# Six reorderings in a two-layer hybrid encoder on one core: refill steps, last-head order, last division on DVE, three weight buffers for the output projections, weights split ahead, scores ahead of transposes

## The chip, the cores and the metric

The kernel runs on one core of one Trainium2 chip. The metric is the device time of one execution in microseconds (us). An execution's time is a little longer than the span of its profile, which runs from the first to the last recorded instruction.

## The reference

Two layers over 1024 tokens of width 1024, all in float32. Layer 0 is a chunk-causal differential attention with eight heads and a squared-ReLU MLP; layer 1 is a sliding-window attention with shared keys and values and a second MLP of the same shape. Cut to what matters here:

```
def attend_block(args):                       # layer 0, for each block of 128 queries
    logits = einsum('bqhcd,bkhcd->bhcqk', q_blk, k) - slopes * dist      # two components c
    p = softmax(where(allowed, logits, -inf))
    wts = p[:, :, 0] - lam * p[:, :, 1]
    return einsum('bhqk,bkhe->bqhe', wts, v)
o = rms_norm(o, subln_g) * (1.0 - lambda_init)         # the division of each head's output
x = x + o @ w_o
x = x + (relu(rms_norm(x, g) @ w_up) ** 2) @ w_down
k, v = rms_norm((rms_norm(x, kv_norm_g) @ w_kv)[...])  # shared keys and values
# layer 1: 16 query heads in 4 groups, a window of two chunks of 64, a sink in each softmax
x = x + windowed_attention(rms_norm(x), k, v) @ w_o
x = x + (relu(rms_norm(x, g) @ w_up) ** 2) @ w_down
```

## The kernel before, in words

**Arithmetic.** Every float32 product is three reduced-precision products on TensorE (PE): high times high, high times low, low times high. So each operand is split once: ACT copies it, rounded, to the high part (`copy`, L952), and DVE subtracts that from the original for the low part (`low`, L1412, or L1413 with a gain). Whatever PE multiplies has gone through ACT and then DVE. Five instruction streams (PE, ACT, DVE, POOL and SP, which issues the DMAs) are written out by hand, each in its own order; semaphores hold them together, and no scheduler moves anything.

**Stages, in order of time.** 0 to 470 us: the first attention, a head at a time, with the projections of the next head between the steps. 470 to 543: its last head (`last_head`), which has no projections left. 543 to 636: the output projection, as eight panels of 128 output channels (`panel_products`; a panel's weights are split by `split_panel` on ACT and DVE, into `w_hi` and `w_lo`, which lie in `w_op`). 636 to 1264: the first MLP. 1264 to 1335: shared keys (job 0) and values (job 1). 1335 to 1563: second attention, four groups whose queries are projected as jobs 2 to 5. 1563 to 1597: the last steps of it, without projections. 1597 to 1686: second output projection. 1686 to 2334: second MLP.

**A step of the first attention.** A step `s` of a head handles 128 queries against 128(s+1) keys. DVE adds the distances and takes the maximum of both components (`maxima`, L1592, tile p) and writes their negative (`nm_a`, L1597); ACT takes both exponentials (`exps`, L1030); DVE forms the coefficient (L1606) and mixes the two (`mix`, L1611); PE transposes the weights into `trb`; ACT and DVE split them into `wT_hi` and `wT_lo`; PE multiplies by the values into `pv`. When all heads are done, outputs are normed per query (on POOL in `norm_steps`, with `chain_o` and `rstd_o`), transposed into oT, which lies in `xT`, and split into `a_hi` and `a_lo`. `EARLY = (7, 3)` says how many heads' outputs are split before the last head is done.

**The MLP.** A product of two 2x2 block matrices is done with seven block products instead of eight; their names are A11, S1, S2, A12, S3, A22, S4. One product takes 12 matmuls into one bank. Operands of x stay in `xop` and `a` (`unit_hi`, `unit_lo`), weights stream through `w_op` (`op_of_weights`, LEAD = 4 products ahead on DVE, 5 on ACT). In the second half (weights down) the operand of u comes back from DRAM: per slice of four outputs, 4 slices in a segment, 14 half-slots of `xop` are loaded (`load_at`) and split again (`refill_hi` on ACT, `refill_lo` on DVE); `refill_at(k)` says in which step of the product loop. `down_add` (L1694) adds a finished bank to `xT`, and frees it.

**The second attention.** Its weights are loaded and split per job (`wb_split` into `wb_hi`, `wb_lo`, eight rows of 128x256, all at a job's boundary). In a step PE transposes q (L2298), transposes the exponentials of the step before (L2315), takes scores (L1958) and multiplies; `Fori(1, KVH - 1)` loops over groups 1 and 2.

## Time and profile before

| what | before |
|---|---|
| time, median of 3 runs | 2344.01 us (2340.61 to 2346.03) |
| time of the profiled execution | 2336.36 us |
| its span | 2334.6 us |
| PE busy | 2213.6 us, 95% |
| DVE, ACT, POOL busy | 1595.2 us (68%), 1162.6 us (50%), 844.4 us (36%) |
| PE's part of the chain that ended last | 80%, DVE 10%, ACT 3% |

The span less the busy time of PE is 121 us, and PE has the largest share of the chain. To see which of those 121 us an edit can touch, each stage is read by itself: windows of the span (busy time of each engine and PE's granted clock, as a share of full speed), PE's waits by what ended them, and the timeline of one engine, in which a square bracket at a row's end tells how long the engine stood idle ahead of it and what released it.

### The profile page before, as it was taken

To read this page: it belongs to the slowest core of one execution; us is meant where nothing else is said; L and a number is where in the kernel's file an instruction comes from. 1 tells how busy PE (TensorE), PEld (TensorE's weight loads), DVE (VectorE), ACT (ScalarE), POOL (GpSimd) and SP (SyncE) were. 2 spreads that over 40 slices of the span, in tenths; PEclk is the share of its full clock that TensorE was granted. 3 is DMA by queue.
4 is the path that set the end of the run, shared out by engine and by line. 5 is a ranking of instruction groups with operands and counts; after the bars stand their busy time and mean duration, and the time that the engine had idled before them with its cause. 6 is when DMAs were issued, how large, how long until landed. Compare 5 with 4: busy or idle time off the path is not lost.

```text
span 2334.6 us, 36548 instructions
## 1 busy us (share of the span) xinstructions
PE 2213.6 (95%) x11916; PEld 1901.1 (81%) x11916; DVE 1595.2 (68%) x3190; ACT 1162.6 (50%) x2484; POOL 844.4 (36%) x1464
## 2 busy tenths in 40 slices
PE   7999999967999999999999989998999999899998
PEld 6899999956878888778777988887878888778777
DVE  6788788763676666876776378874676666876773
ACT  5566666653555555543344256654555555543342
POOL 3333333334633322233344155553633322233331
PEclk9999999968999999999999999998999999999999
DMA  6111110002434444663352100003434445663352
GB/s 203 31 28 28 27 27 22 2 28 96 130 103 158 157 151 165 247 229 106 129 198 91 37 20 20 0 20 109 126 113 152 153 150 171 237 232 103 132 172 81
DMA packets 186628, 255.86 MB, mean 110 GB/s; under 512 B 14944, under 2 KB 135776, under 8 KB 181856
## 3 DMA queue, kind: packets, MB, share of 16 engines
q1 hardware_dynamic: 186464, 253.82, 32.8%
q8 instruction: 86, 1.41, 0.3%
q14 instruction: 78, 0.64, 0.1%
HBM read 174.09 MB, written 79.69 MB: 109 GB/s over the span
## 4 chain that ended last, share of the span: by engine, by line
PE 80%; DVE 10%; issue 4%; ACT 3%; DMA 1%; POOLq 1%; POOL 0%; DVEq 0%; SPq 0%; ACTq 0%
PE score L1958 45%; PE trb L1958 13%; PE proj L1958 13%; PE pv L1958 5%; DVE xop L1412 3%; DVE w_op L1412 1%; PE trb L1999 1%; PE trb L2315 1%; ACT p L1030 1%; DVE xT L1694 1%; DVE p L1592 1%; DMA w_quad<-in_mlp_w_down 1%; DVE pb L1905 1%; DVE wb_lo L1413 1%; ACT pb L1377 1%
## 5 line engine op out<-in xcount | busy, mean ns | idle before, releaser
L1958 PE MATMUL score<-xop,w_op 128*128 128x512 f32 x3840 | 893.6, 391 | 24.0 <-DVE xop L1412 12.9
L1958 PEld LDWEIGHTS score<-xop,w_op 128*128 128x128 f32 x3840 | 720.9, 189 | 183.6 <-issue 34.5
L828 POOL TENSOR_TENSOR w_quad<-w_quad,w_sum 128x512 f32<-128x512 f32 x64 | 99.6, 1557 | 806.9 <-DVE w_op L1412 806.9
L1958 PE MATMUL trb<-xop,w_op 128*128 128x512 f32 x1536 | 361.8, 390 | 5.7 <-DVE w_op L1412 1.7
L1958 PEld LDWEIGHTS trb<-xop,w_op 128*128 128x128 f32 x1536 | 287.5, 188 | 68.9 <-issue 6.3
L952 ACT ACTIVATE w_op<-w_quad 128x512 fp32r<-128x512 f32 (+1 forms) x336 | 216.3, 646 | 246.6 <-PE score L1958 167.5
L1412 DVE TENSOR_TENSOR w_op<-w_quad,w_op 128x512 fp32r<-128x512 f32 (+1 forms) x336 | 284.3, 850 | 45.5 <-ACT w_op L952 45.5
L1694 DVE TENSOR_TENSOR xT<-score,xT 128x512 f32<-128x512 f32 x160 | 110.0, 687 | 158.5 <-PE score L1958 150.0
L1958 PE MATMUL score<-a_hi,w_op 128*128 128x512 f32 x512 | 160.8, 394 | 3.8 <-DVE w_op L1412 3.8
L1030 ACT ACTIVATE p<-p,nm_a,slopes 128x128 f32<-128x128 f32 (+7 forms) x124 | 106.5, 861 | 112.8 <-DVE nm_a L1597 110.7
L1412 DVE TENSOR_TENSOR xop<-xop 128x1024 fp32r<-128x1024 f32 x112 | 142.5, 1284 | 14.3 <-ACT xop L952 14.3
L952 ACT ACTIVATE quad<-score 128x512 f32<-128x512 f32 x96 | 57.3, 597 | 186.8 <-PE score L1958 178.2
L1958 PE MATMUL proj<-wa_hi,a_hi 128*128 128x384 f32 x418 | 142.8, 342 | 0.8 <-DVE v_parts L1413 0.8
L1958 PE MATMUL proj<-wa_hi,a_lo 128*128 128x384 f32 x418 | 140.0, 335 | 0.0
L1958 PE MATMUL proj<-wa_lo,a_hi 128*128 128x384 f32 x418 | 139.7, 334 | 0.0
L952 ACT ACTIVATE w_op<-w_sum 128x512 fp32r<-128x512 f32 x128 | 77.0, 627 | 107.7 <-PE score L1958 50.8
L1694 DVE TENSOR_TENSOR quad<-trb,quad 128x512 f32<-128x512 f32 x64 | 44.2, 690 | 110.0 <-PE trb L1958 76.1
L952 ACT ACTIVATE xop<-xop 128x1024 fp32r<-128x1024 f32 x112 | 115.7, 1046 | 5.4 <-DMA xop<-u_dram 5.4
L1958 PEld LDWEIGHTS score<-a_hi,w_op 128*128 128x128 f32 x512 | 97.5, 190 | 24.9 <-DVE w_op L1412 4.3
L471 POOL TENSOR_TENSOR chain_p<-rstd_qk 128x8 f32<-128x8 f32 x96 | 19.9, 208 | 245.7 <-DVE rstd_qk L463 236.3
L1592 DVE CUSTOM_DVE_ANT_0 p<-score,dist_a 128x128 f32<-128x128 f32 (+7 forms) x124 | 88.7, 752 | 29.2 <-PE score L1958 29.2
L1958 PE MATMUL proj<-wb_hi,b_hi 128*128 128x256 f32 x320 | 98.2, 307 | 6.8 <-DVE wb_lo L1413 5.8
(285 smaller groups left out, 4564.2 us busy)
## 6 DMA issues: line engine op xcount, KB each, us to landing
xop<-u_dram SPq DMA_DIRECT2D x112, 512.0 KB, 5.6
u_dram<-quad SPq DMA_DIRECT2D x32, 1536.0 KB, 9.6
w_quad<-in_mlp_w_up SPq DMA_DIRECT2D x64, 512.0 KB, 5.5
w_quad<-in_mlp_w_down SPq DMA_DIRECT2D x64, 512.0 KB, 4.9
wa_raw<-in_a_w_qkv SPq DMA_DIRECT2D x96, 128.0 KB, 2.5
quad<-xT_dram SPq DMA_DIRECT2D x32, 256.0 KB, 4.1
xT_dram<-xs SPq DMA_DIRECT2D x32, 256.0 KB, 2.6
u_dram<-quad SPq DMA_DIRECT2D x32, 256.0 KB, 3.8
```

The source lines that it names most:

```text
L828: return pool.tensor_tensor(out, x, y, ALU.subtract)
L952: return nc.scalar.activation(out, in_, ACT.Copy, scale=scale)
L1030: nc.scalar.activation(p[:, 0:keys], p[:, 0:keys], ACT.Exp, bias=nm_a[i][:, c:c + 1], scale=one(slopes, h), accum_out=ssum[par][:, c, s:s ...
L1377: nc.scalar.activation(pb[par][:, j, lo:256], pb[par][:, j, lo:256], ACT.Exp, bias=nm_b[par][:, j:j + 1], accum_out=sm_b[par][:, j:j + 1])
L1412: return nc.vector.tensor_tensor(out, full, hi.bitcast(F32), ALU.subtract)
L1413: return nc.vector.scalar_tensor_tensor(out=out, in0=full, scalar=scale, in1=hi.bitcast(F32), op0=ALU.mult, op1=ALU.subtract)
L1592: nc.vector.tensor_tensor_reduce(out=p[:, 0:keys], in0=score[c][:, 0:keys], in1=dist_a[:, S - keys:S], scale=1.0, scalar=LOWEST, op0=ALU.a ...
L1694: return nc.vector.tensor_tensor(out, a, b, ALU.add)
L1905: nc.vector.tensor_tensor_reduce(out=pb[par][:, j, lo:256], in0=score_cols(j, lo), in1=bias_b[:, j, lo:256], scale=1.0, scalar=LOWEST, op0 ...
L1958: return nc.tensor.matmul(out, a, b, start=start, stop=stop, **kw)
L1999: last = nc.tensor.transpose(trb[b][:, P * (kc - 4 * i):P * (kc - 4 * i + 1)], p0[block_s % 2][:, P * kc:P * (kc + 1)], ident[:, :])
L2315: last = nc.tensor.transpose(trb[b][:, P * j:P * (j + 1)], pb[s % 2][:, j, P * b:P * (b + 1)], ident[:, :])
```

## The change

1. Refills: the list of steps, of whose 14 entries the first three stay and eleven go one product earlier; in the loop over products both refills go to the head, on ACT ahead of all else in a step, on DVE right behind `down_add`.
2. Last head: each component's maximum is announced by itself, ACT starts the first exponential behind the first; ACT's `wT_hi` of a step goes ahead of the next exponentials; the panel splits and the squares move, and the low parts of seven heads' outputs go from POOL to DVE, behind the head.
3. The last division: nine small instructions and one multiply, on DVE instead of POOL.
4. Panels: three buffers and three pairs of PSUM banks instead of two, splits one panel further ahead; the early products of panels 0 and 1 first with `a_hi` alone; the last panel half by half.
5. `wb_split` in pieces, six of eight rows ahead of the job's boundary (odd jobs in other memory, `wb_rows`).
6. Second attention, steps without projections (`full` false): PE's scores ahead of the transposes of the weights, DVE's maxima ahead of their low parts.
7. The loop over groups 1 and 2 is written out.

```
-    steps = (1, 2, 4, 5, 6, 7, 8, 8, 9, 10, 11, 11, 12, 13)
+    steps = (1, 2, 4, 4, 5, 6, 7, 7, 8, 9, 10, 10, 11, 12)
...
+        w_hi = [w_op[:, i, :, :].rearrange("p a (k n) -> p (a k) n", n=P) for i in (2, 0, 5)]
+        w_lo = [w_op[:, i, :, :].rearrange("p a (k n) -> p (a k) n", n=P) for i in (3, 1, 6)]
...
+        wo_bank = [bank[0], bank[1], [proj[:, :], pv[:, :]]]
...
+        def rsqrt_steps_dve(dve, out, vec, t, n):
+            v, t = vec[:, 0:n], t[:, 0, 0:n]
+            for i in range(3):
+                if i:
+                    dve.drain()
+                dve.scalar_tensor_tensor(out=t, in0=v, scalar=-0.5, in1=out, op0=ALU.mult, op1=ALU.mult)
+                dve.drain()
+                dve.tensor_tensor(t, t, out, ALU.mult)
+                dve.drain()
+                last = dve.scalar_tensor_tensor(out=out, in0=t, scalar=1.5, in1=out, op0=ALU.add, op1=ALU.mult)
+            return last
...
+        def wb_rows(part, k, job):
+            if job % 2 and k < 6:
+                return wo_b[:, k // 2, part, 256 * (k % 2):256 * (k % 2 + 1)]
+            return (wb_hi, wb_lo)[part][:, k, :]
...
-            pool.wait_ge(qkv_ready, NH * NB)
-            split_early(0)
-            pool.wait_ge(o_rstd, NH)
-            norm_steps(rstd_o[:, :], chain_o, NB)
-            o = head_out[1]
-            pool.tensor_tensor(o, o,
-                               rstd_o[:, :].unsqueeze(2).to_broadcast([P, NB, P]), ALU.mult).then_inc(o_normed, 1)
...
+                def last_exps(s):
+                    keys, i = P * (s + 1), s % 2
+                    act.sem_inc(act_passed, 1)
+                    for c, p in ((0, p0[i]), (1, p1s[i])):
+                        act.wait_ge(nm_ready, h * NB + 2 * s + c + 1)
+                        nc.scalar.activation(p[:, 0:keys], p[:, 0:keys], ACT.Exp, bias=nm_a[i][:, c:c + 1],
+                                             scale=one(slopes, h),
+                                             accum_out=ssum[par][:, c, s:s + 1]).then_inc(exp_done, 1)
...
+                last_exps(0)
+                high_wT(uses, 0)
+                for s in range(NB - 1):
+                    high_wT(uses, s + 1)
+                    last_exps(s + 1)
...
+            high_early(5)
+            act.drain()
             square_outputs(NH * 4, 1, NB - 2)
+            high_early(6)
+            split_panel(2)
...
                 for k in range(OPS + 6):
+                    for s, h in refill_at(k):
+                        refill_hi(s, h)
...
                         op_of_weights(k + LEAD + 1)
-                    for s, h in refill_at(k):
-                        refill_hi(s, h)
...
+                def both_maxima(s):
+                    for c in range(2):
+                        if c:
+                            dve.wait_ge(mixed, h * NB + max(s - 1, 0))
+                        one_maximum(s, c)
...
+            dve.wait_ge(o_normed, NH - 1)
+            dve.drain()
+            rsqrt_steps_dve(nc.vector, rstd_o[:, :], chain_o, chain_p, NB)
+            dve.drain()
+            nc.vector.tensor_tensor(head_out[1], head_out[1],
+                                    rstd_o[:, :].unsqueeze(2).to_broadcast([P, NB, P]), ALU.mult).then_inc(o_normed, 1)
+            for c in range(EARLY[0]):
+                dve.wait_ge(o_early_hi, c + 1)
+                low(a_lo[:, c, :], oT[:, c, :], a_hi[:, c, :]).then_inc(o_split, 1)
+            split_panel(2)
...
+                    for s, h in refill_at(k):
+                        refill_lo(s, h)
                     if k < 4:
...
+                    full = proj_on and (s < NB - 1 or more)
+                    def low_weights_b():
+                        for b in range(2):
+                            if ("p", s, b) in uses:
+                                dve.wait_ge(bm_hi[b], uses["p", s, b] + 1)
+                                low(wTb_lo[:, b, :], trb[b][:, :], wTb_hi[:, b, :]).then_inc(bm_free[b], 1)
+                    if full:
+                        low_weights_b()
...
+                    pe.wait_ge(o_early_hi, k + 1)
+                    for i in range(2):
+                        x_h = a_hi[:, k, HALF * i:HALF * (i + 1)]
+                        mm(wo_bank[slot][i], w_hi[slot][:, k, :], x_h, k == 0, False)
+                        mm(wo_bank[slot][i], w_lo[slot][:, k, :], x_h, False, False)
+                    if slot and k == 2:
+                        transpose_outputs(last_uses, NH, 1)
+            for slot in range(2):
+                for k in range(EARLY[0]):
                     pe.wait_ge(o_split, k + 1)
-                    panel_products(slot, a_hi, a_lo, k)
-                if slot == 0:
-                    transpose_outputs(last_uses, NH, 1)
+                    for i in range(2):
+                        mm(wo_bank[slot][i], w_hi[slot][:, k, :], a_lo[:, k, HALF * i:HALF * (i + 1)], False, False)
 ...
-                    if i >= 2:
-                        pe.wait_ge(xs_ready, 16 * seg + 2 * i - 2)
+                    if i >= 3:
+                        pe.wait_ge(xs_ready, 16 * seg + 2 * i - 4)
+                    if i == KC - 1:
+                        last_panel(i % 3)
...
+            def last_panel(slot):
+                out, w_h, w_l = wo_bank[slot], w_hi[slot], w_lo[slot]
+                for k in range(KC):
+                    last = three(out[1], (w_h[:, k, :], w_l[:, k, :]), (a_hi[:, k, HALF:S], a_lo[:, k, HALF:S]),
+                                 k == 0, k == KC - 1)
+                last.then_inc(panel_half, 1)
+                for k in range(KC):
+                    mm(out[0], w_h[:, k, :], a_hi[:, k, 0:HALF], k == 0, False)
+                    last = mm(out[0], w_l[:, k, :], a_hi[:, k, 0:HALF], False, False)
+                    if k in (3, KC - 1):
+                        last.then_inc(wo_half, 1)
+                for k in range(KC):
+                    last = mm(out[0], w_h[:, k, :], a_lo[:, k, 0:HALF], False, k == KC - 1)
+                last.then_inc(panel_half, 1)
...
+                        if s in (2, 3, 4, NB - 2) and more:
+                            wb_split(g + 3, 4, *((6, KC) if s == NB - 2 else (2 * s - 4, 2 * s - 2)))
...
-            with act.Fori(1, KVH - 1) as g:
+            for g in range(1, KVH - 1):
...
+                    if not full:
+                        transpose_weights_b()
```

The order of instructions on ACT in the last head, before, around its seventh step's exponentials (p_0 and p are the two components of step 6, p_1 and p_last those of step 7, `w_op` a panel's weights, `sq_a` squares):

```order
L1030 ACTIVATE p_0,ssum<-p_0,nm_a,slopes 128x896
L1030 ACTIVATE p,ssum<-p,nm_a,slopes 128x896
L1139 ACTIVATE sq_a,oss<-oraw 128x128 x2
L952 ACTIVATE wT_hi<-trb 128x512
L952 ACTIVATE wT_hi<-trb 128x256
L952 ACTIVATE w_op<-w_quad 128x1024
L952 ACTIVATE a_hi<-xT 128x1024
L1030 ACTIVATE p_1,ssum<-p_1,nm_a,slopes 128x1024
L1030 ACTIVATE p_last,ssum<-p_last,nm_a,slopes 128x1024
L952 ACTIVATE wT_hi<-trb 128x512
L952 ACTIVATE wT_hi<-trb 128x384
```

The same place in the changed kernel:

```order
L1078 ACTIVATE p_0,ssum<-p_0,nm_a,slopes 128x896
L1078 ACTIVATE p,ssum<-p,nm_a,slopes 128x896
L969 ACTIVATE a_hi<-xT 128x1024
L1172 ACTIVATE sq_a,oss<-oraw 128x128 x2
L969 ACTIVATE w_op<-w_quad 128x1024
L969 ACTIVATE wT_hi<-trb 128x512
L969 ACTIVATE wT_hi<-trb 128x384
L1078 ACTIVATE p_1,ssum<-p_1,nm_a,slopes 128x1024
L1078 ACTIVATE p_last,ssum<-p_last,nm_a,slopes 128x1024
```

The weights of step 6 (the `wT_hi` of 384 columns) are now split ahead of step 7's exponentials and no longer behind them.

On DVE in the first slice of refills (`xT` is a `down_add`, `w_op` a weights' low part, `xop` a refill's), before:

```order
L1694 TENSOR_TENSOR xT<-score,xT 128x512
L1412 TENSOR_TENSOR w_op<-w_quad,w_op 128x512
L1412 TENSOR_TENSOR xop<-xop 128x2x512
L1694 TENSOR_TENSOR xT<-trb,xT 128x512
L1694 TENSOR_TENSOR xT<-score,xT 128x512
L1412 TENSOR_TENSOR w_op<-w_quad,w_op 128x512
L1412 TENSOR_TENSOR xop<-xop 128x2x512 x2
```

and in the changed kernel:

```order
L1772 TENSOR_TENSOR xT<-score,xT 128x512
L1458 TENSOR_TENSOR xop<-xop 128x2x512 x2
L1458 TENSOR_TENSOR w_op<-w_quad,w_op 128x512
L1772 TENSOR_TENSOR xT<-trb,xT 128x512
L1772 TENSOR_TENSOR xT<-score,xT 128x512
L1458 TENSOR_TENSOR xop<-xop 128x2x512
L1458 TENSOR_TENSOR w_op<-w_quad,w_op 128x512
```

A refill's low part now stands ahead of the weights' low part of its step, and the pair stands one product earlier, ahead of the two `down_add` of the next product.

On DVE in a step without projections (`mx_b` are the maxima, `wTb_lo` the weights' low part, `osb` the outputs of the step before), before:

```order
L1933 TENSOR_TENSOR osb<-osum,rc_b 128x256
L1412 TENSOR_TENSOR qTb_lo<-score,qTb_hi 128x256
L1412 TENSOR_TENSOR wTb_lo<-trb,wTb_hi 128x512 x2
L1905 ISA pb,mx_b<-score,bias_b 128x192
L1905 ISA mx_b 128x1
```

and in the changed kernel the end of the same step:

```order
L2000 TENSOR_TENSOR mx_b<-mx_b,sinks 128x4
L2002 TENSOR_TENSOR esin_b<-sinks,mx_b 128x4
L2003 TENSOR_SCALAR nm_b<-mx_b 128x4
L1458 TENSOR_TENSOR wTb_lo<-trb,wTb_hi 128x512 x2
L2015 TENSOR_TENSOR den_b<-sm_b,es_b 128x4
```

The weights' low parts went from ahead of the maxima to behind them.

## Rows read from the trace of the kernel before

**Rows 1.** Page, part 1: busy us, share of the span, instructions of each engine.

```profile
PE 2213.6 (95%) x11916; PEld 1901.1 (81%) x11916; DVE 1595.2 (68%) x3190; ACT 1162.6 (50%) x2484; POOL 844.4 (36%) x1464
```

**Rows 2.** Windows: length, then busy PE, PEld, DVE, ACT, POOL; PEclk, DMA share, GB/s.

```profile
470.00:543.00 73.00, 45.72 (x230) 36.56 (x229) 46.26 (x101) 34.81 (x83) 28.65 (x42) 0.63 0.15 44
935.00:977.00 42.00, 36.46 (x152) 28.72 (x151) 35.75 (x45) 27.89 (x41) 9.71 (x6) 0.96 0.79 288
1303.00:1315.00 12.00, 10.24 (x73) 10.07 (x72) 6.02 (x21) 4.98 (x13) 1.50 (x6) 0.86 0.21 65
```

**Rows 3.** Timeline of DVE, last head: start, length, instruction, [idle before, releaser].

```profile
477.63 0.35 DVE L1611 SCALAR_TENSOR_TENSOR p<-p,coef_a,p 128x128 f32<-128x128 f32 x1
...
523.83 1.21 DVE L1592 CUSTOM_DVE_ANT_0 p<-score,dist_a 128x1024 f32<-128x1024 f32 x1
...
529.65 1.16 DVE L1412 TENSOR_TENSOR wT_lo<-trb,wT_hi 128x512 fp32r<-128x512 f32 x2 [2.60 <-ACT wT_hi L952]
530.97 1.23 DVE L1412 TENSOR_TENSOR w_op<-w_quad,w_op 128x1024 fp32r<-128x1024 f32 x1 [0.17 <-ACT w_op L952]
...
533.44 2.22 DVE L1611 SCALAR_TENSOR_TENSOR p<-p_last,coef_a,p 128x1024 f32<-128x1024 f32 x1
```

**Rows 4.** Timeline of ACT, last head's step 7.

```profile
526.58 1.24 ACT L1030 ACTIVATE p<-p,nm_a,slopes 128x1024 f32<-128x1024 f32 x1 [6.30 <-DVE nm_a L1597]
...
529.05 0.95 ACT L952 ACTIVATE wT_hi<-trb 128x512 fp32r<-128x512 f32 x2
```

**Rows 5.** Timeline of DVE, the last mix of the head before.

```profile
470.18 1.28 DVE L1611 SCALAR_TENSOR_TENSOR p<-p,coef_a,p 128x1024 f32<-128x1024 f32 x1
```

**Rows 6.** Timeline of PE, first panels of the output projection.

```profile
569.17 0.53 PE L1958 MATMUL score<-a_hi,w_op 128*128 128x512 f32 x1 [3.83 <-DVE w_op L1412]
```

**Rows 7.** The chain that ended last, in order of time: start, length, work.

```profile
569.17 69.87 PE score L1958 x300
...
668.95 13.60 PE score L1958 x60
```

**Rows 8.** Timeline of PE, start of each MLP.

```profile
643.61 7.32 PE L1958 MATMUL score<-xop,w_op 128*128 128x512 f32 x24 [1.85 <-issue]
...
1711.25 3.00 PE L1958 MATMUL trb<-xop,w_op 128*128 128x512 f32 x12 [1.73 <-DVE w_op L1412]
```

**Rows 9.** PE's waits, 640 to 1264 us: total us, times, longest.

```profile
PE score L1958 <- DVE xop L1412: 6.5, 4, 3.2
```

**Rows 10.** Timeline of DVE, two refills' low parts of the second slice.

```profile
1031.58 1.22 DVE L1412 TENSOR_TENSOR xop<-xop 128x1024 fp32r<-128x1024 f32 x1
...
1035.68 2.32 DVE L1412 TENSOR_TENSOR xop<-xop 128x1024 fp32r<-128x1024 f32 x1
```

**Rows 11.** Page, part 6, DMA issues: count, KB each, us to landing.

```profile
xop<-u_dram SPq DMA_DIRECT2D x112, 512.0 KB, 5.6
```

**Rows 12.** PE's waits, 1290 to 1345 us, then 1345 to 1563.

```profile
PE pv L1958 <- DVE wb_lo L1413: 1.8, 1, 1.8
PE proj L1958 <- DVE wb_lo L1413: 1.6, 1, 1.6
...
PE proj L1958 <- DVE wb_lo L1413: 4.2, 3, 1.4
```

**Rows 13.** PE's waits, 1563 to 1598 us.

```profile
PE trb L2315 <- ACT es_b L1379: 5.9, 3, 2.3
...
PE score L1958 <- DVE qTb_lo L1412: 2.0, 1, 2.0
```

**Rows 14.** Timeline of PE, two steps in the loop and the same two in group 3.

```profile
1467.60 1.22 PE L2315 MATMUL trb<-ident,pb 128*128 128x128 f32 x8 [1.26 <-DVE kTb_lo L1413]
...
1481.08 1.09 PE L2315 MATMUL trb<-ident,pb 128*128 128x128 f32 x8 [0.51 <-ACT es_b L1379]
...
1528.70 1.22 PE L2315 MATMUL trb<-ident,pb 128*128 128x128 f32 x8 [1.06 <-DVE kTb_lo L1413]
...
1542.07 1.09 PE L2315 MATMUL trb<-ident,pb 128*128 128x128 f32 x8 [0.39 <-ACT es_b L1379]
```

More of the change, by code:

```diff
@@ L1199, in squares @@
                 def squares(i):
-                    for half in range(2):
+                    if i == KC - 1:
+                        act.wait_ge(panel_half, 2 * KC * (seg + 1))
+                    for half in halves_of(i):
                         if i % 2 and i < KC - 1:
@@ L1830, in segment @@
                         factors()
-                    for s, h in refill_at(k):
-                        refill_lo(s, h)
                     if seg == 0:
@@ L2383, in _ @@
             steps(0, False, True, range(NB))
-            with pe.Fori(1, KVH - 1) as g:
+            for g in range(1, KVH - 1):
                 steps(g, True, True, range(NB))
```

281 lines of the change are left out of this document (152 added, 129 removed).

## The prediction

> **What bounds the kernel now.** First the page's busy times: PE works 2213.6 us, 95% of the span, and DVE, the next, 68% [rows 1]. Outside of PE's own work only 2334.6 - 2213.6 = 121 us are left, and a part of PE's busy time is stretched by a lower clock. Then windows, to find where those lie [rows 2]. In the last head PE is busy 45.7 of 73 us at a mean granted clock of 0.63: it waits there for a circle of other engines. In a slice of refills (935 to 977) it stands 42 - 36.5 = 5.5 us, at 0.96; around the boundary of jobs (1303 to 1315) 1.8 us, at 0.86. The reader is to see that a stop costs twice: the idle time, and a time behind it in which the clock is down. I price each stage by its own waits and its own clock.
>
> The sum is made against the profiled execution, 2336.4 us; the median of the runs shown is 7.6 us above it, and I add that at the end.
>
> **A. Last head: 15 us.** From the end of the first mix (477.63 + 0.35 = 477.98) to the end of the last (533.44 + 2.22 = 535.66) seven steps take 57.7 us [rows 3]. This is a circle mix, maxima, exponentials, weights' split, coefficient, mix. What leaves it:
> - The second maximum. The first of step 7 ends at 523.83 + 1.21 = 525.04 [rows 3]; ACT starts the exponential at 526.58, having waited for nm_a, the two maxima's common result [rows 4]. 1.5 us, of which I take 1.15, since the announcement itself stays. It grows with the number of keys (0.34 in step 1), and over seven steps sums to 5.2.
> - Weights' split behind the exponentials. wT_hi runs at 529.05 [rows 4], wT_lo 529.65 to 530.8, and the coefficient can't start before [rows 3]. Summed over the steps 8.5 us. As the split goes ahead of the exponentials, PE's transposes and wT_hi enter the circle there, partly beside the first maximum: I take 3 back, so 5.5.
> - One of the two panel splits (the 1.23 at 530.97 of step 7; in the new order that of step 7 stays and the other goes behind the loop) 1.3, and squares on ACT 1.5.
> - POOL beside DVE. The mix over 1024 columns takes 2.22 in the last head [rows 3] and 1.28 in the head before [rows 5]; POOL was making the low parts of the seven outputs there, and these move behind the head. 0.94 for this one; with the smaller excesses of the other mixes, coefficients and low parts in the head I estimate 4.3.
>
> That is 17.8. PE's transposes run here at the low clock and gain a place in the circle, so I take 2 to 3 off: 15, bounds 10 and 19.
>
> **B. Join to the panels: 5.7 us.** At 569.17 PE waited 3.83 us for the low part of panel 2's weights [rows 6], since two buffers only let its split begin late. With three buffers it stands ahead of that. Behind the stop 300 matmuls took 69.87 us; at 13.60/60 = 0.2267 each they would take 68.0 [rows 7], so 1.9 more. The division on DVE I cost at nothing. Its cover is the 56 matmuls of panels 0 and 1 with high parts alone, 12.7 us at 0.2267; seven low parts are then wanted behind it, which DVE can begin some 6 us after the last values are there (my estimate from nine steps of a quarter microsecond and a multiply of 1.2), and takes 7 x 1.2 = 8.4 for. They come at about 557, the last is wanted at about 559: 2 us are left. If the cover were gone, each microsecond of lateness would be one of the end.
>
> **C. Starts of the MLPs: 6 us.** In the first, PE stood 1.85 us and then took 7.32 for 24 matmuls, where 24 x 0.2267 = 5.4 would do [rows 8]; with a further 0.5 stop some 4.0. In the second the same 1.85, 0.2, and 1.73 for a weights' low part [rows 8]: 3.7. The last panel's new order lets the operands be split half by half ahead of its end. It also puts four weights' low parts of DVE ahead of the second half's addition, so of 7.7 I take 6; bounds 2 and 7.7.
>
> **D. Refills: 11 us.** The waits for a refill's low part are 6.5 us in the first MLP, in four stops, the longest 3.2 [rows 9], and the same in the second, plus 0.8. The window 935 to 977 is the first slice: 5.5 us of stops and 0.04 x 42 = 1.7 of clock [rows 2]. There ACT's refill stood behind a weights' split whose own load came late; ahead of it, it doesn't wait. I take 4.5 of 7.2 for each MLP's first slice, 9. In the other three slices a refill's low part takes 1.22 or 2.32, the second when POOL works beside it [rows 10]. Two such in one step now stand ahead of the next product's additions into xT, which free PE's bank: 2 x 2.32 = 4.6 us against a product of 12 x 0.2267 = 2.7, so the bank comes about 1.9 late, where the old order waited 1.6. So those slices give little, 2 of some 6.6 in all. Together 11; bounds 4 and 18 (nothing in slice 0 beyond the one long stop; everything).
>
> The trace has that same row as evidence for the price of POOL's neighbourhood, 2.32 against 1.22 [rows 10]. The Trainium skill, page "SBUF — State Buffer", section "Who interferes with whom", says more: a DVE instruction with both inputs in SBUF contends with a GpSimd instruction that reads SBUF, and the loser waits for the whole of the other's instruction. A refill's low part has both inputs in SBUF, a low part from PSUM has not. By it every refill that meets a weights' sum of POOL would be doubled, and D would fall to its lower bound, 4; by the row, only those that the new place brings there, and D is 11.
>
> **E. Weights split ahead: 9 us.** PE waits for wb_lo 1.8, 1.6 and three times 1.4: 7.6 us [rows 12]. Clock behind the stops: 0.14 x 12 = 1.7 at 1303 to 1315 [rows 2], 0.9 at another by the same reading. Two rows of eight still are split at the boundary, and take some 1 back. What pays: steps 2 to 4 get two rows each, on ACT and DVE, which have room there. Sum 9; bounds 6 and 10.2.
>
> **F. Steps without projections: 2 us lost.** PE's transposes waited 5.9 us for the exponentials with the scores queued behind them [rows 13], which looks as though scores ahead would win. But the scores waited 2.0 for qTb_lo as well [rows 13], and the next step's exponentials hang on maxima that gain at most 0.5 to 1.3 once. Against it the weights' low parts now stand behind four maxima, with pv behind them, and this in four steps. Bounds: gain 0.5, loss 3.
>
> **G. The loop written out: 0.** The same two steps take 1481.08 - 1467.60 = 13.48 us in the loop and 1542.07 - 1528.70 = 13.37 straight [rows 14].
>
> Sum: 15 + 5.7 + 6 + 11 + 9 - 2 + 0 = 44.7. 2336.4 - 44.7 = 2291.7, and with 7.6 the median is **2299**. A measurement of this kernel tells 0.2%, 4.7 us, from no change.
>
> **The rivals.**
> - *The refills' waits only move* (chance 0.18). By the 2.32 row, refills at the head of the queue meet POOL and hold the additions. D gives nothing, or 1: 44.7 - 10.7 = 34, time 2310. For it: that row, and three slices whose bank comes late by my own working. Against: POOL is busy only 9.7 of 42 us in a slice [rows 2].
> - *PE at the low clock bounds the last head* (0.1). With other waits gone, PE's pair, outputs and weights transposes at 0.63 of the clock set the steps; A gives 7.5 less, time 2307. For it: 0.63 in 73 us [rows 2], and that PE stands 27 us of them. Against: if the head gets shorter, PE is busier in it. The Trainium skill, "TensorE: Matmul & The Clock Gate", section "What's actually happening", says that "the default state is throttled, and activity releases the throttle": by it a denser head would raise the clock and A would near 19.
> - *Everything in full* (0.2): 17.8 + 5.7 + 7.7 + 17 + 10.2 and nothing lost in F is 58.4, time 2286. For it: each is the trace's own wait. Against: waits of a chain seldom vanish without another that stood 1 to 2 us behind.
> - *Slower* (0.03). One mechanism: refills at the head of ACT's and DVE's queues wait for their own load. A load lands 5.6 us after issue [rows 11] and is now wanted 2 products, 5.4 us, after it, eleven of fourteen times. Each late microsecond then holds DVE's additions, and so PE. With 56 refills per MLP in pairs, 56 pairs in all: 1 us late each costs 56, and D's 11 isn't won: 33.7 - 56 = -22, time 2366. The turning point is 33.7/56 = 0.6 us per pair. Against: PE needs the freed bank two products later, and weights are split four products ahead, 10.9 us, which covers several such waits.
>
> **How the numbers follow.** The main case, 2292 to 2306, gets 0.4, the four rivals 0.51, and 0.09 is for mixtures with a gain of 10 to 30 us or of more than 60. Likeliest is 2299. The range from 2279 to 2320 takes in "in full" (2286) with the bounds of the terms beneath it, and 2310 with a further 10 for a lost C and F. Faster by over 0.2%: 0.95; within 0.2%: 0.02; slower: 0.03.
>
> **What would show it.** A: the mixes of steps 1 to 7 apart by 50 us less some (42.7 in place of 57.7), the last mix about 1.3 us long, the exponential beginning right behind the first maximum. B: no row of PE waiting for w_op after the join, and no wait for a_lo ahead of the 28 late matmuls. C: stops ahead of the MLPs' first products under 1 us. D: in 935 to 977 less than 3 us idle; in the later slices xop rows of 2.32 and PE waiting for DVE's xT. E: no waits for wb_lo above 0.5. F: PE waiting for wTb_lo or expb over 2 us in the steps without projections. The prediction is wrong if the head's steps hang on something I left out (PE's outputs of head 6 inside the circle), or if loads reach the head of ACT's queue late.

## The result and the profile after

The changed kernel takes 2310.8 us (median of 4 runs, 2306.0 to 2314.2), the kernel before 2342.3 beside it: a ratio of 0.9865, interval 0.9835 to 0.9895, so 1.35% or 31.5 us faster. The profiled execution took 2313.9 us, near the top of that spread, with a span of 2312.1; the profiled execution of before, 2336.4, lies below the median of its runs. So between the two profiles lie 22.5 us and not 31.5, and the ledger below is made of those 22.5.

The page, part 1 of the changed kernel, answers to [rows 1]; then the groups of part 5 for the refills on ACT and on DVE (busy, mean ns, idle before and what ended it), and their loads from part 6, which answer to [rows 11]:

```profile
PE 2205.3 (95%) x11916; PEld 1899.8 (82%) x11916; DVE 1603.9 (69%) x3215; ACT 1159.5 (50%) x2484; POOL 819.6 (35%) x1433
...
L1458 DVE TENSOR_TENSOR xop<-xop 128x1024 fp32r<-128x1024 f32 x112 | 145.8, 1317 | 11.4 <-ACT xop L969 11.2
...
L969 ACT ACTIVATE xop<-xop 128x1024 fp32r<-128x1024 f32 x112 | 116.9, 1052 | 72.5 <-DMA xop<-u_dram 72.3
...
xop<-u_dram SPq DMA_DIRECT2D x112, 512.0 KB, 5.8
```

PE still is busy 95% of a shorter span. What is new is the third row: ACT stands 72 us ahead of the refills for their loads, where it stood 5 before, though a load lands in 5.8 us where it did in 5.6.

Stretches between the same instructions of both profiles show where the time went (for the first row the end of a mix, for the others the start of a row of PE):

| stretch | before | after | gain | the prediction's term |
|---|---|---|---|---|
| last head, first mix to last mix | 57.7 | 39.2 | 18.5 | A 15 |
| last mix to PE's last product of the head | 3.5 | 3.2 | 0.3 | |
| to the MLP's third group of products | 122.3 | 114.4 | 7.9 | B 5.7 and C's 4.0 |
| first MLP, to the first product of keys | 610.6 | 617.6 | -7.0 | D |
| keys, values, groups 0 to 3 with projections | 270.0 | 258.8 | 11.2 | E 9, G 0 |
| steps without projections | 54.9 | 59.3 | -4.4 | F -2 |
| second panels, to the same place of the second MLP | 114.3 | 114.3 | 0.0 | C's second part |
| second MLP, to the transposes of the outputs | 616.8 | 620.3 | -3.6 | D |

The first of these stretches begins 0.5 us later than before; 22.9 - 0.5 is the 22.5 us between the spans, but for rounding. Each gain is that of one profile. Where the experiments run the same code in a stretch, their profiles give its spread, and this is told beside the term below.

**Last head.** The timeline of DVE after: the first mix, the first maximum of step 7, the last mix. They answer to [rows 3].

```profile
478.11 0.35 DVE L1658 SCALAR_TENSOR_TENSOR p<-p,coef_a,p 128x128 f32<-128x128 f32 x1
...
510.20 1.22 DVE L1679 CUSTOM_DVE_ANT_0 p<-score,dist_a 128x1024 f32<-128x1024 f32 x1
...
516.36 1.28 DVE L1658 SCALAR_TENSOR_TENSOR p<-p_last,coef_a,p 128x1024 f32<-128x1024 f32 x1
```

The mix takes 1.28 us where it took 2.22, and begins 6.2 us after the maximum, where it was 9.6. ACT's timeline, which answers to [rows 4]: the exponential now begins behind the weights' split, with no idle time, and not right behind the first maximum, as the prediction had it.

```profile
511.14 0.95 ACT L969 ACTIVATE wT_hi<-trb 128x512 fp32r<-128x512 f32 x2
511.99 1.23 ACT L1078 ACTIVATE p<-p,nm_a,slopes 128x1024 f32<-128x1024 f32 x1
```

PE's windows from the first mix to the head's last product, before and then after, show the clock (the column behind POOL) risen from 0.58 to 0.77:

```profile
478.00:539.00 61.00, 36.69 (x170) 28.36 (x168) 40.05 (x81) 31.70 (x73) 28.07 (x40) 0.58 0.11 35
```

```profile
478.00:521.00 43.00, 30.86 (x175) 25.39 (x175) 35.59 (x90) 30.95 (x72) 8.88 (x27) 0.77 0.06 18
```

**Join and division.** DVE's timeline, the last division's multiply, then the low parts (a row groups overlapping ones); and PE's first product with one of them, which has no bracket:

```profile
527.77 1.23 DVE L1757 TENSOR_TENSOR oraw<-oraw,rstd_o 128x1024 f32<-128x1024 f32 x1
528.92 3.49 DVE L1458 TENSOR_TENSOR a_lo<-xT,a_hi 128x1024 fp32r<-128x1024 f32 x3
```

```profile
536.48 6.51 PE L2049 MATMUL score<-a_lo,w_op 128*128 128x512 f32 x28
```

PE asks at 536.5 for what DVE began at 528.9, and has no stop between 520.9 and 623.9: the 3.83 us of [rows 6] are gone. At the MLPs' starts a wait for a weights' low part stays, which answers to [rows 8]:

```profile
635.21 3.00 PE L2049 MATMUL trb<-xop,w_op 128*128 128x512 f32 x12 [1.35 <-DVE w_op L1458]
...
1685.21 4.57 PE L2049 MATMUL trb<-xop,w_op 128*128 128x512 f32 x12 [2.01 <-DVE w_op L1458]
```

In the second row 12 matmuls take 4.57 us instead of 3.00. These 1.6 us of lower clock, right behind a stop of 2.0, fall into the second MLP's row of the table, though no refill has run yet.

**Refills.** All engines in the second slice of the first MLP, after (it answers to [rows 10]):

```profile
1005.23 1.06 ACT L969 ACTIVATE xop<-xop 128x1024 fp32r<-128x1024 f32 x1 [3.57 <-DMA xop<-u_dram]
...
1006.32 4.54 DVE L1458 TENSOR_TENSOR xop<-xop 128x1024 fp32r<-128x1024 f32 x2 [0.78 <-ACT xop L969]
...
1007.62 2.16 POOL L843 TENSOR_TENSOR w_quad<-w_quad 128x512 f32<-128x512 f32 x1
...
1010.79 1.76 DVE L1458 TENSOR_TENSOR w_op<-w_quad,w_op 128x512 fp32r<-128x512 f32 x1
...
1012.47 0.68 DVE L1772 TENSOR_TENSOR xT<-trb,xT 128x512 f32<-128x512 f32 x1
...
1013.07 0.68 DVE L1772 TENSOR_TENSOR xT<-score,xT 128x512 f32<-128x512 f32 x1
```

```profile
1013.85 11.53 PE L2049 MATMUL score<-xop,w_op 128*128 128x512 f32 x37 [3.67 <-issue]
```

To be read from above: ACT stands 3.57 us for a load, and DVE waits 0.78 of these for ACT; the two low parts take 4.54 us together, where two of 1.22 would take 2.4, since POOL is at work; the weights' low part behind them takes 1.76 where it takes 0.69 without POOL; only then come the two additions that free PE's banks, and PE starts 0.1 us after the second. The bracket says "issue" because the profile saw nothing end the wait, but the time points to the addition. There are six stops of this kind, of 2.4 to 3.7 us, in slices 2 to 4 of the two MLPs, where before each slice had one of 0.5 and one of 1.1.

Whether such a stop is of 2.4 us or of 3.6 hangs on who starts first. Here POOL's sum into `w_sum` began 0.07 us ahead of DVE's first low part. At the next slice DVE began 0.03 us ahead of the same sum:

```profile
1006.25 1.29 POOL L857 TENSOR_TENSOR w_sum<-w_quad 128x512 f32<-128x512 f32 x1
```

```profile
1089.13 3.47 DVE L1458 TENSOR_TENSOR xop<-xop 128x1024 fp32r<-128x1024 f32 x2 [0.69 <-ACT xop L969]
...
1089.16 2.35 POOL L857 TENSOR_TENSOR w_sum<-w_quad 128x512 f32<-128x512 f32 x1
```

There the two low parts took 3.47 us and PE stood 2.43. In all 42 such stops, six in each of seven profiles with these refills, it is so: with the sum ahead the stop is of 3.59 us or more, with DVE ahead of 2.36 to 2.45.

And a window of the slice of the 3.67 us stop:

```profile
1010.00:1092.00 82.00, 78.33 (x333) 64.47 (x333) 54.03 (x71) 29.87 (x42) 22.53 (x16) 0.96 0.41 137
```

0.04 x 82 = 3.3 us more, at the lower clock behind the stop.

**Second attention.** From 1290 to 1545 no wait for wb_lo is left, where [rows 12] had five. In the steps without projections, PE's timeline, which answers to [rows 13], and then DVE and POOL at the same place:

```profile
1540.82 0.36 PE L2049 MATMUL score<-kTb_hi,qTb_hi 64*128 64x192 f32 x2 [2.60 <-DVE qTb_lo L1458]
...
1545.48 0.45 PE L2049 MATMUL pv<-vb,wTb_hi 128*128 128x128 f32 x1 [2.38 <-DVE wTb_lo L1458]
...
1553.67 0.54 PE L2049 MATMUL score<-kTb_hi,qTb_hi 64*128 64x192 f32 x2 [3.66 <-DVE qTb_lo L1458]
```

```profile
1544.06 1.27 DVE L1458 TENSOR_TENSOR wTb_lo<-trb,wTb_hi 128x512 fp32r<-128x512 f32 x2
...
1545.19 2.35 POOL L804 TENSOR_TENSOR a_lo<-xT,a_hi 128x1024 fp32r<-128x1024 f32 x1
1545.26 2.30 DVE L2015 TENSOR_TENSOR den_b<-sm_b,es_b 128x4 f32<-128x4 f32 x1
```

The transposes lost their waits for es_b, but the scores wait for qTb_lo now, and pv 2.38 us for the low parts that went behind the maxima.

The stretch of keys, values and groups, 258.8 us here, takes 258.7 to 264.6 us in ten other profiles with the same code in it. The difference to the changed kernel's own profile lies mostly in PE's clock while the keys are made: 0.83 in their first 20 us here, 0.57 in e1 and before. Windows of this stretch, before, after, and in e1:

```profile
1272.09:1542.07 269.98, 248.56 (x2088) 236.54 (x2089) 184.04 (x672) 139.05 (x459) 120.12 (x429) 0.96 0.07 24
```

```profile
1252.82:1511.62 258.80, 240.71 (x2089) 229.43 (x2089) 186.06 (x672) 139.01 (x459) 122.56 (x429) 0.99 0.08 25
```

```profile
1250.62:1513.58 262.96, 245.67 (x2088) 234.11 (x2088) 185.69 (x672) 139.02 (x459) 122.53 (x429) 0.96 0.07 25
```

At the clock of before, 0.96, the gain is 7.0 us and not 11.2.

### The profile page after: what moved, and what is told of

It reads as the page before. It is cut to its first block, busy times and chain, and to the rows that moved or that the text cites. A ratio compares the mean times of both kernels' runs of the same rounds, so it can differ in the third digit from the quotient of the medians.

```text
span 2312.1 us, 36311 instructions
## 1 busy us (share of the span) xinstructions
PE 2205.3 (95%) x11916; PEld 1899.8 (82%) x11916; DVE 1603.9 (69%) x3215; ACT 1159.5 (50%) x2484; POOL 819.6 (35%) x1433
## 4 chain that ended last, share of the span: by engine, by line
PE 76%; DVE 11%; issue 5%; DMA 3%; ACT 2%; DVEq 1%; POOLq 1%; POOL 0%; ACTq 0%; SPq 0%
PE score L2049 41%; PE proj L2049 13%; PE trb L2049 13%; PE pv L2049 6%; DMA xop<-u_dram 3%; DVE xop L1458 2%; DVE w_op L1458 2%; PE trb L2090 1%; DVE pb L1994 1%; PE trb L2428 1%; ACT p L1047 1%; DVE wTb_lo L1458 1%; ACT xop L969 1%; PE trb L2144 0%; DVE osum L2021 0%
## 5 line engine op out<-in xcount | busy, mean ns | idle before, releaser
L843 POOL TENSOR_TENSOR w_quad<-w_quad,w_sum 128x512 f32<-128x512 f32 x64 | 89.0, 1390 | 799.6 <-DVE w_op L1458 799.6
L1458 DVE TENSOR_TENSOR xop<-xop 128x1024 fp32r<-128x1024 f32 x112 | 145.8, 1317 | 11.4 <-ACT xop L969 11.2
L969 ACT ACTIVATE xop<-xop 128x1024 fp32r<-128x1024 f32 x112 | 116.9, 1052 | 72.5 <-DMA xop<-u_dram 72.3
L1047 ACT ACTIVATE p<-p,nm_a,slopes 128x128 f32<-128x128 f32 (+7 forms) x112 | 96.4, 862 | 90.0 <-DVE nm_a L1644 90.0
L2049 PE MATMUL score<-a_hi,w_op 128*128 128x512 f32 x384 | 114.4, 395 | 0.0
L857 POOL TENSOR_TENSOR w_sum<-w_quad 128x512 f32<-128x512 f32 x64 | 97.8, 1528 | 32.8 <-DMA w_quad<-in_mlp_w_up 20.9
L1639 DVE CUSTOM_DVE_ANT_0 p<-score,dist_a 128x128 f32<-128x128 f32 (+7 forms) x112 | 80.3, 754 | 29.3 <-PE score L2049 29.3
L843 POOL TENSOR_TENSOR w_quad<-w_quad 128x512 f32<-128x512 f32 x64 | 95.3, 1488 | 5.0
```

Source lines behind the costliest of these rows:

```text
L843: return pool.tensor_tensor(out, x, y, ALU.subtract)
L857: pool.tensor_tensor(w_full(n, "S1"), quarter(n, 1, 0), quarter(n, 1, 1), ALU.add)\
L969: return nc.scalar.activation(out, in_, ACT.Copy, scale=scale)
L1047: nc.scalar.activation(p[:, 0:keys], p[:, 0:keys], ACT.Exp, bias=nm_a[i][:, c:c + 1], scale=one(slopes, h), accum_out=ssum[par][:, c, s:s ...
L1458: return nc.vector.tensor_tensor(out, full, hi.bitcast(F32), ALU.subtract)
L1639: nc.vector.tensor_tensor_reduce(out=p[:, 0:keys], in0=score[c][:, 0:keys], in1=dist_a[:, S - keys:S], scale=1.0, scalar=LOWEST, op0=ALU.a ...
```

## The experiments

The times are medians; "ratio" is to the kernel before on the same chip, with its interval. "MLP stretches" are the fourth row of the table above, and for the second MLP the time from its third group of products to a fixed early row of the output's transposes (before 548.7, after 552.3).

**e1, e2, e3: the refills' place and steps, undone together and one by one.**

```
-    steps = (1, 2, 4, 4, 5, 6, 7, 7, 8, 9, 10, 10, 11, 12)
+    steps = (1, 2, 4, 5, 6, 7, 8, 8, 9, 10, 11, 11, 12, 13)      # e1, e3
...
-                    for s, h in refill_at(k): refill_hi(s, h)     # e1, e2: to behind op_of_weights,
-                    for s, h in refill_at(k): refill_lo(s, h)     # on ACT and on DVE
```

> The changed kernel with the refills as they were: their old steps, and at the end of a step of the product loop on ACT and DVE. In the profile of the changed kernel the first MLP takes 609.9 us from its third group of products to its last (602.7 before) and the second 613.4 (609.8 before). Theory 1, the new place and steps of the refills cost those 10.7 us: both come back, so 10 to 12 us less than the changed kernel, some 2300, and ACT's idle time ahead of the refills that a load ended falls from 72 to under 10. Theory 2, the three buffers and the new start of the MLP changed the rhythm, and the refills are innocent: within 3 us of the changed kernel.

> The changed kernel with the new, earlier steps of the refills, but again at the end of a step, behind the split of the weights. Theory 1a, it is the place at the head of the queues that costs (ACT waits there for a load with the weights behind it): 8 to 12 us less than the changed kernel, and ACT's wait for loads under 30 us. Theory 1b, it is the earlier steps (a load has 2 products of 2.7 us to land in, and lands after 5.8): it stays within 4 us, with the waits for loads still 50 us or more, since the refill of a step is wanted as early.

> The changed kernel with the old, later steps of the refills, but at the head of the queues. Theory 1a (the place costs): no gain, within 4 us of the changed kernel. Theory 1b (the steps cost): 8 to 14 us less than the changed kernel; a load then has a product more, 8.2 us instead of 5.4, so ACT's wait for loads falls below 15 us, and the stops of PE of 2.2 to 3.7 us go. It may even beat the kernel with all refills as before, by some of the 3.2 us stop in each first slice, since there ACT's refill stood behind a split of weights that had come late.

| | time us | ratio | MLP stretches | ACT's wait for loads |
|---|---|---|---|---|
| old place, old steps (e1) | 2309.5 | 0.9857 (0.9841 to 0.9873) | 614.4 + 550.7 | 5.1 |
| old place, new steps (e2) | 2307.4 | 0.9855 (0.9837 to 0.9873) | 615.7 + 550.9 | 14.0 |
| new place, old steps (e3) | 2296.0 | 0.9811 (0.9797 to 0.9824) | 608.6 + 543.4 | 49.3 |
| new place, new steps (after) | 2310.8 | 0.9865 (0.9835 to 0.9895) | 617.6 + 552.3 | 72.3 |

The groups of ACT and DVE in e3:

```profile
L1458 DVE TENSOR_TENSOR xop<-xop 128x1024 fp32r<-128x1024 f32 x112 | 144.7, 1303 | 6.4 <-ACT xop L969 6.4
...
L969 ACT ACTIVATE xop<-xop 128x1024 fp32r<-128x1024 f32 x112 | 116.7, 1050 | 49.3 <-DMA xop<-u_dram 49.3
```

e1 gave no gain in time, against theory 1. e2 stays within 4 us of the changed kernel, as theory 1b has it, but with 14 us of waits for loads and not 50 or more. e3 was the one that came out: 14.8 us under the changed kernel by the medians, 12.6 by the ratios, each to its own runs of the kernel before (2342.3 and 2340.5). So neither "the edits cost" nor "the edits are innocent" holds: the place at the head of the queues pays some 13 us, but only with the later steps, and one product earlier takes it all back. e3's ACT still waits 49 us for loads, more than the 15 expected, and it does no visible harm: in e3's slices 2 to 4 the stops of 2.4 to 3.7 us are gone, and one of 1.1 each is left. What tells is where DVE's additions stand. In e2's second slice, with hardly a wait for a load, the pair of low parts is ahead of them, as in the changed kernel, and PE stands 2.21 us; in e3 they are ahead of the pair. DVE in e2, then in e3:

```profile
1010.18 4.55 DVE L1458 TENSOR_TENSOR xop<-xop 128x1024 fp32r<-128x1024 f32 x2
...
1014.66 0.68 DVE L1772 TENSOR_TENSOR xT<-trb,xT 128x512 f32<-128x512 f32 x1
```

```profile
1009.18 0.67 DVE L1772 TENSOR_TENSOR xT<-score,xT 128x512 f32<-128x512 f32 x1
1009.78 3.44 DVE L1458 TENSOR_TENSOR xop<-xop 128x1024 fp32r<-128x1024 f32 x2
```

So the late load is not what makes these stops; it adds to them, by the 0.4 to 0.8 us that DVE stands ahead of the pair in the changed kernel, and by more where POOL's sum gets in first.

**e4: the steps without projections in their old order**, PE and DVE.

```
-                    elif prev: transpose_q()
+                    else: transpose_both()
...
-                    if full: low_weights_b()
+                    low_weights_b()
```

> The changed kernel with the old order in the second attention's steps without projections: on PE the transposes of the weights ahead of the scores, on DVE the weights' low parts ahead of the maxima. From the last transposes of group 3 to the last outputs these steps take 59.3 us in the changed kernel and 54.9 before. If the order is what costs: 4.4 us less than the changed kernel, and this stretch 55. If the stretch grew for another reason (the panel's split, weights in other buffers): no difference, and the stretch stays at 59.

2309.0 us, ratio 0.9868 (0.9852 to 0.9883); the stretch takes 54.7 us, against 59.3 in the changed kernel. The order is what cost 4.6 us. In the whole time it doesn't show, which varies by more.

**e5 to e7: parts of the last head; e8: the division.**

```
-   act.wait_ge(nm_ready, h * NB + 2 * s + c + 1)
+   act.wait_ge(nm_ready, h * NB + 2 * s + 2)        # e5
...
-   high_wT(uses, s + 1); last_exps(s + 1)
+   last_exps(s + 1); high_wT(uses, s + 1)           # e6
```

e7 moves the seven `a_lo` subtractions from behind the head on DVE to POOL's queue behind `run_heads`; e8 gives POOL `norm_steps` and the multiply again.

> The changed kernel, but in the last head ACT starts the first exponential only when both maxima are announced, as before. Seven steps from the end of the first mix to that of the last take 39.2 us in the changed kernel's profile, 36.3 to 37.2 in four variants with the same code there, and 57.7 before. Theory 1, the second maximum was in the circle with its length: 4 to 5 us more in this stretch (the prediction's term of 5.2). Theory 2, after the weights' split went ahead of the exponentials these wait for that split and not for a maximum: under 1.5 us more.

> The changed kernel, but in the last head ACT splits the weights of a step behind the next exponentials again. Theory 1, the split's place gives the prediction's 5.5 us: the stretch of seven steps grows by 4 to 7 us, and the exponentials start right behind the first maximum. Theory 2, the two are complements (with the split behind, the first exponential starts earlier, at the first maximum): 1 to 3 us.

> The changed kernel, but POOL makes the low parts of the seven heads' outputs during the last head, as before, and DVE none of them behind it. Theory 1, POOL's reads slowed DVE's instructions with both inputs in SBUF: the mix over 1024 columns goes from 1.28 to some 2.2 us again, and the stretch of seven steps grows by 3 to 5 us. Theory 2, the mixes that were long before were so by chance or by the panel splits: the mixes stay at 1.28 and the stretch within 1 us. Nothing is lost at the join, where the low parts are there earlier.

> The changed kernel with the last division on POOL again, 6.4 us there instead of 3.6 on DVE. The early products need only high parts in 12.7 us. Theory 1, the division is hidden either way: no difference in the stretch from the last head's last product to the MLP's third group (114.4 to 115.9 us in five profiles), DVE starting the low parts 3 us earlier. Theory 2, it is late for the transposes of head 7's outputs, which now stand between the early products: a wait of PE of 1 us or more there.

| | time us | ratio | seven steps | head's last product to MLP |
|---|---|---|---|---|
| after | 2310.8 | 0.9865 | 39.2 | 114.4 |
| eight others, same code in the head | | | 36.3 to 37.2 | 114.3 to 115.9 without e8 |
| e5 | 2323.4 | 0.9918 (0.9892 to 0.9944) | 41.1 | 116.8 |
| e6 | 2319.2 | 0.9906 (0.9882 to 0.9929) | 44.4 | 114.4 |
| e7 | 2316.7 | 0.9899 (0.9876 to 0.9922) | 39.0 | 116.4 |
| e8 | 2321.2 | 0.9924 (0.9903 to 0.9945) | 36.4 | 122.7 |

The whole times lie further apart than the stretches, since the MLPs with the changed refills vary by themselves: 1161 to 1173 us together in seven profiles of the same code. I read these four from the stretches. e5: 4 to 5 us against the eight others, 1.9 against the changed kernel's own; the second maximum was in the circle. e6: 7 to 8 us (5.2 against the changed kernel's own), and the exponentials start right behind the first maximum, so theory 1, if anything by more than its 4 to 7. e7: the join to the MLP is 0.5 us above the others' 115.9, nearly nothing as expected; the last mix takes 2.23 us again and the coefficient ahead of it 1.00 instead of 0.22, but the three other mixes that were long before (1.68 to 2.08) stay short, and the stretch grows by 1.7 to 2.7 us, or not at all against the changed kernel's own. DVE's timeline of e7:

```profile
508.15 1.15 DVE L1666 SCALAR_TENSOR_TENSOR p<-p,coef_a,p 128x896 f32<-128x896 f32 x1
...
516.17 2.23 DVE L1666 SCALAR_TENSOR_TENSOR p<-p_last,coef_a,p 128x1024 f32<-128x1024 f32 x1
```

e8 fell out against theory 1. PE and then POOL in e8:

```profile
536.43 1.97 PE L2120 MATMUL trb<-ident,oraw 128*128 128x128 f32 x8 [6.30 <-POOL oraw L835]
```

```profile
523.61 0.20 POOL L478 TENSOR_TENSOR chain_p<-rstd_o 128x8 f32<-128x8 f32 x1 [30.46 <-DVE rstd_o L470]
523.77 1.21 POOL L480 TENSOR_SCALAR chain_p<-chain_o 128x8 f32<-128x8 f32 x1
...
533.06 0.20 POOL L478 TENSOR_TENSOR chain_p<-rstd_o 128x8 f32<-128x8 f32 x1
...
534.49 1.90 POOL L835 TENSOR_TENSOR oraw<-oraw,rstd_o 128x1024 f32<-128x1024 f32 x1
```

Instructions on eight columns take 0.2 us alone and 0.95 to 1.21 while DVE makes the low parts, and the division 12.8 us in all instead of 6.4. In this order of work the division on DVE is worth 7 to 8 us (122.7 against 114.3 to 115.9), not nothing.

**e9: e3 and e4 together; e10: of e3's place only ACT's.**

> The changed kernel with two parts undone: the old steps of the refills (kept at the head of the queues) and the old order in the steps without projections. Theory 1, the two add: 14.8 from the first and 4.6 from the second, so some 2291 where the kernel before runs at 2340, a ratio of 0.979. Theory 2, part of the first was chance in the MLPs (their stretches vary by 5 us between runs of one code): 2297 or more.

> The old steps of the refills, on ACT at the head of the queue, on DVE behind the weights' low part as before. Theory 1, ACT's place is what pays (a refill no longer stands behind a weights' split whose load came late): the two MLP stretches sum to within 3 us of the 1152 with both at the head. Theory 2, DVE's place pays (the 1.1 us stops for xop, and the stops of 3 us): they sum to 1160 or more, as with both as before (1165).

e9: 2289.9 us, ratio 0.9798 (0.9785 to 0.9811), stretches 606.7 + 543.6 and 54.7: the two add, and it is the fastest kernel of the study. Its page, part 1:

```profile
PE 2201.2 (96%) x11916; PEld 1895.8 (83%) x11916; DVE 1612.5 (70%) x3215; ACT 1159.6 (51%) x2484; POOL 818.5 (36%) x1433
```

e10: 2302.7 us, ratio 0.9845 (0.9830 to 0.9860), stretches 609.4 + 547.2 = 1156.6, between the two theories: ACT's place gives some 8.5 of the 13, DVE's the rest, by one profile each, where e3 and e9, of the same code in the MLPs, are 1.8 apart (the stops of 1.1 us come in pairs with one of 0.4 to 0.5 again).

**e11: weights of a job in one piece.**

```
-                if s == 5:
-                    wb_split(1, 3, 0, 6)
-            wb_split(1, 3, 6)
+            wb_split(1, 3)                          # and so for the other jobs
```

> The changed kernel with all eight rows of a job's weights split at the job's boundary, still with the odd jobs' first six rows in the other memory. Theory 1, the pieces gave what the stretches show between before and after (from the first product of keys to the last transposes of group 3: 270.0 against 258.8): it takes 9 to 12 us more than the changed kernel there, with waits for wb_lo of 1.4 to 1.8 us at five boundaries. Theory 2, the gain came from the loop being written out or from the buffers: under 3 us.

2323.4 us, ratio 0.9927 (0.9910 to 0.9944). The stretch of the second attention takes 269.9 us, as before the change. PE's waits from 1240 to 1565, where the odd jobs' rows are called wo_b:

```profile
PE proj L2041 <- DVE wb_lo L1455: 3.0, 2, 1.6
...
PE proj L2041 <- DVE wo_b L1455: 2.7, 2, 1.4
...
PE pv L2041 <- DVE wo_b L1455: 1.8, 1, 1.8
```

7.5 us in five waits. Against the 258.7 to 264.6 of the profiles with the pieces this is 5 to 11 us, and 7.0 against e1, whose clock in this stretch is like that of e11: the pieces gave the whole of the gain, the loop written out nothing.

**e12: the kernel before, refills first, old steps.**

```
                 for k in range(OPS + 6):
+                    for s, h in refill_at(k): refill_hi(s, h)     # refill_lo on DVE behind down_add
...                                                       # the same two loops at the step's end are gone
```

> The kernel before with one edit alone: both refills at the head of a step's work, at their old steps. In the changed kernel this edit (old steps) took the two MLP stretches from 1165 to 1152 us. Theory 1, the place pays by itself and needs nothing else of the change: 10 to 15 us less than the kernel before, a ratio of about 0.995, and both stretches together 1146 to 1150 (1159 before). Theory 2, it needs the new start of the MLP or was chance: within 3 us of before.

2327.7 us against 2337.7, ratio 0.9955 (0.9941 to 0.9969), stretches 606.5 + 542.5 = 1149.0. Theory 1: the place pays 10 us by itself and needs nothing of the rest.

No run puts back the third panel buffer or the order of the last panel (B and C), nor the places of the panel split and the squares (in A).

## Why the prediction came out as it did

The time lies in the range and 12 us over the likeliest; of the cases it is that of "the refills' waits only move", 2310. That the number came so near is partly chance, since errors of both signs cancelled: A, B and C's first part, and E came to 37.9 in the profile where 33.7 had been forecast, D to -10.6 where 11 had. The prediction's own sign of being wrong, "if loads reach the head of ACT's queue late", came with 72 us of such waits.

- **A, 15, measured 18.5** (20.4 to 21.4 by the eight others). The second maximum, forecast 5.2, is 2 to 5 (e5). The weights' split, forecast 5.5 after 3 taken back, is 5 to 8 (e6). POOL's part, forecast 4.3, is at most 2.7 (e7): only one mix was slowed by it. The 2 to 3 taken off for PE at the low clock were not needed: in the shorter head the clock rose from 0.58 to 0.77, against the rival of PE at the low clock. No experiment stands for the panel split and the squares.
- **B, 5.7, and C's first part, 4.0: 7.9 together.** The wait at the join is gone. The wait for w_op ahead of the MLP's third group came in place of what stood there, 1.35 us. No run takes the third buffer back; that it did this is read from the missing wait alone. "The division on DVE I cost at nothing" was right for the sum, since nothing waited, but the division had a cover only because it moved. Left on POOL it costs 7 to 8 us (e8).
- **C's second part: 0.** The stops fell from 3.7 to 2.9 us, but the first 20 us of the second panels ran at a clock of 0.86 against 0.92 before. The new order of the steps ahead of them doesn't explain it: that window has 0.93 in e3 and 0.86 in e1, both with the new order, and 0.92 in e4 and 0.87 in e9, both with the old. The windows, before and then after:

```profile
1597.00:1617.00 20.00, 20.00 (x83) 16.48 (x84) 8.27 (x8) 8.63 (x11) 4.78 (x5) 0.92 0.68 217
```

```profile
1571.00:1591.00 20.00, 20.00 (x79) 16.41 (x80) 9.41 (x9) 9.57 (x12) 4.78 (x5) 0.86 0.68 213
```

- **D, 11, measured -10.6: the step that failed.** Two terms of it did. In the first slices I took 4.5 us each; PE's stops there fell from 5.5 to 4.6 us and from 7.1 to 4.0. For the other slices I had worked out that two contended low parts put the bank 1.9 us late, set that against 1.6 of before, and still took a gain of 2; the stops there went from 9.1 us in all to 18.1, with the lower clock behind them. I left out the weights' low part between the pair and the additions, 1.76 us where it takes 0.69 alone, and the wait for the load in front, 0.4 to 0.8 us, which the "slower" rival had. The pair itself was right as the worst case: 3.5 to 4.5 us against my 4.6.

  Not all of the 10.6 is the refills' doing. e1, which has them as before, stands 5.8 us above the kernel before in the two MLPs together. 1.6 us in each are the clock behind the stop ahead of the third group of products, C's matter and not D's (in the changed kernel's own profile only the second MLP has them); 2.3 and 0.4 are longer stops in the first slices. What the runs showed of the refills themselves is an interplay: the place alone gains 13 (1165 to 1152), the steps alone lose 1.5, and both together lie between a gain of 4 and a loss of 8 in seven profiles, 3 lost in their mean. With the place alone the additions come ahead of the pair where these stops were (e3); with the new steps the pair is ahead, in either place (e2). e12 shows that my reading of the first slice was right for the place.

  Contention did not strike every refill: the mean of a refill's low part is 1.32 us, where it was 1.28. My sum had two slips: "everything" is 7.2 twice and 6.6, 21 and not 18 or 17; and by my list of steps only 24 steps of both MLPs have a pair, not 56, so the 56 of the "slower" rival does not stand.
- **E, 9, measured 11.2**, and 5.4 to 11.2 by the eleven profiles with this code: the size was right, and all of it is the pieces (e11). The changed kernel's own profile gives the upper end, since its keys ran at the higher clock. **G, 0**, holds: with the loop written out and the split in one piece the stretch is what it was.
- **F, -2, measured -4.4**: the mechanism was right, the size off. The order is what cost it (e4). PE waited for the low parts that stand behind the maxima; besides, POOL's making of a_lo met a tiny instruction of DVE (2.30 us for one on four columns), whose share no run separates.

**Open:** why the first slice of e1 has 2.3 us more of stops in the first MLP than the kernel before (7.9 against 5.5, the largest 3.65 for DVE's addition into xT), and why the clock in the keys and in the second panels differs between profiles of the same code.

## What to carry to other kernels

Moving an instruction to the head of a queue and moving it to an earlier step are two edits, and should be timed as two. Here the first paid, in the first slices because a weights' split ahead of the refill was late itself; the second paid in neither place. Ahead of such a move look at what will stand behind the instruction on its own queue, above all the operation that frees a bank, and add up everything between the two, at the lengths that the other engines leave it. A load that lands later than the new distance in products adds to that, but an idle wait ahead of an instruction costs nothing if nothing behind it is wanted yet. And an edit that looks free because nothing waited for it before can be what makes another edit possible; undo it in the new kernel before calling it free. Last, one profile gives a stretch only to within its own spread: take the same stretch from every variant that leaves its code alone before naming a cause for a microsecond.

## What the runs showed of the hardware

In these rows contention between DVE and POOL strikes short instructions hardest. POOL's instructions on eight columns went from 0.20 us to between 0.95 and 1.21 beside DVE's subtractions of 1.2 us (e8), and DVE's addition on four columns took 2.30 us beside POOL's subtraction of 2.35, where it takes 0.16 alone. The Trainium skill, page "SBUF — State Buffer", section "Who interferes with whom", has the rule: with two inputs in SBUF on DVE and a read on POOL, the loser waits for the whole of the other's instruction. The trace agrees: each short instruction lasts about as long as one long one of the other engine.

Which of two instructions that begin within 0.1 us is the longer one can be a matter of hundredths: POOL's sum took 1.3 us where it began ahead of DVE's low part, and 2.3 to 2.4 where it began behind it, and PE's stop was of 3.6 us or of 2.4 with it, in all 42 cases.
